# The token mixer of a two-block kernel, rewritten as a pipeline of dense steps with attention, index and recurrent groups between their units

## The chip, the cores and the metric

The kernel runs on one core of one Trainium2 chip, as one program. A core has a matrix engine (PE, TensorE, whose weight loads stand apart as PEld), a vector engine (DVE), a scalar engine (ACT), GpSimd (POOL) and a queue engine (SP) that here only issues weight transfers. The engines run side by side, each takes its own instructions in order, and they wait for one another on semaphores. The metric is device microseconds of one execution, as the median of the runs. Times inside the program are counted from the first instruction of the profiled execution.

## The reference, cut to what matters

Two transformer blocks run one after the other on 256 tokens of width 1024, all in float32. The change touches only the `token_mixer` of the second block:

```
proj = xn @ w_in
(qa, ka, va, qb, kb, vb, qi, ki, wi, xc, yc, gates) = split(proj)
y_a = moba_attention(qa, ka, va)            # causal softmax attention, 8 heads of 64, with a distance bias
y_b = dsa_attention(qb, kb, vb, qi, ki, wi) # the same, over the 64 keys that the index scores pick
y_c = rg_lru(causal_depthwise_conv(xc, conv_w, conv_b), ...) * gelu(yc)
g = sigmoid(gates).reshape(B, S, 3, D)
merged = g[:, :, 0] * (y_a @ w_pa) + g[:, :, 1] * (y_b @ w_pb) + g[:, :, 2] * (y_c @ w_pc)
return merged @ w_o
```

The index scores are `sum_h wi[h] * relu(qi[h] . ki)` over 8 heads, and a query keeps its 64 best keys. After the mixer come a residual sum, a norm and an MLP.

## The kernel before

**Dense steps.** Each weight matrix is worked off in steps. A step is 4 units (`SLOTS`) of 256 rows by 512 columns of the weight, 512 KB each. SP loads a unit into `raw`. ACT rounds it to `wh` (L1377), and DVE makes the rest `wl = raw - wh` (L2014). PE then makes three products for each tile (`three`, L550 to L554: high by high, high by low, low by high). `unit_used` counts the units that PE is done with, `lo_done` those that DVE has ready. A step "f" writes features by tokens (192 matmuls for two steps of 256 columns each way), a step "t" tokens by features. So while PE works on one step, ACT and DVE prepare the next one, unit by unit, each unit after PE has let go of its slot.

**PSUM in two halves.** Every step, and every group of small matmuls, takes the next half of PSUM (4 of 8 banks) by `open_group`, which waits until the half was emptied two groups ago (`emptied`, ticked by a one-element memset on DVE, L2036). So a small group between two steps has to be read out before the step after the next group can start.

**The mixer's order on PE** (L1243 to L1349): the steps qa, ka, va, qb, kb, vb, qi, kw (only 72 columns: ki and wi), xc, yc, then the transposition of the keys (L1256), gate step 0, the recurrence's gates (L1266), the index scores (L1279) with gate step 1 between their two tiles, and then the attention. It has four rounds n: 0 and 1 are the two halves of the heads of the first attention, 2 and 3 those of the second. A round is: scores (L1293), bias, mask and row maxima on DVE (`maxima`, L2726), exponentials on ACT (`softmax`, L1929), division on DVE (`normalise`, L2748), transposition of the probabilities on PE (L1303 to L1305), copies by ACT and DVE, product with the values (L1321). One gate step stands in each round. After the rounds come three steps `w_pa`, `w_pb`, `w_pc` (L1338 on), each multiplied by its gates on DVE (L2787) and summed (L2790), then 16 transposes of the sum (L1345), and two steps of `w_o`.

**DVE's own work** in the mixer: the weighted sum of the index scores (L2688 to L2695, 8 heads for each tile), the choice of the 64 best in two halves of four rounds (`choose`, L2719 to L2722), the convolution (L2661), the recurrent scan (L2708), the biases, maxima and divisions. The order on each engine is written out by hand: DVE and ACT call `split()` for all four units of the next step, then read out the step that just ended (`read_half`, `read_values`, `take_gate`).

ACT holds one table of functions at a time. Going from an exponential to a sigmoid or back is an ACT_TABLE_LOAD in its row of instructions.

Of the kernel before, what the change touches and what calls it, by code (L numbers as in the profile page):

```python
# [176 lines left out]
def build(nc, a, out):  # L177
    ctx = ExitStack()
    with ctx:
# [109 lines left out]
        rt, it = area(45, 4, SEQ), area(49, 4, SEQ)  # L289
        la, lt = area(53, 4, SEQ), area(57, 4, SEQ)  # L290
        wri = area(61, 2, 4, 64)
# [3 lines left out]
        gates3 = [area(kb, 2, 2, 512) for kb in (63, 37, 71)]  # L295
# [111 lines left out]
        merged = sem("merged")  # L407
        gain_loaded, out_ready = sem("gain_loaded"), sem("out_ready")
# [13 lines left out]
        def _(sp):  # L422
# [90 lines left out]
            with sp.Fori(0, 7) as i:  # L513
                S.enter(i, 1)
                load(cols(w, i * 512))
            S.leave(7)
            load(cols(w, W2["kw"], 72))
            with sp.Fori(0, 8) as i:
                S.enter(i, 1)
                load(cols(w, i * 512 + W2["xc"]))  # L520
            S.leave(8)
# [17 lines left out]
        def _(pe):  # L539
# [703 lines left out]
            for n, kind in enumerate("fftfftf"):  # L1243
                if kind == "f":
                    step_features(SEQ, fresh=n == 0)
                else:
                    step_tokens(range(2))
            step_tokens(range(2), 72)
            keys = G.now()
            step_features(SEQ)  # L1250
            conv = G.now()
            step_features(SEQ)
            pe.wait_ge(emptied, keys)
            hb = open_group()
            for t in range(2):
                mm = pe.transpose(ps[:, hb, t * P:(t + 1) * P], ki2[:, t, :], ident[:, :])  # L1256
            mm.then_inc(turned, 1)
            keys = G.now()
            step_tokens(range(2))
            pe.wait_ge(mix_loaded, 64)  # L1260
            pe.wait_ge(emptied, conv)
            hb = open_group()
            for z in range(2):
                for b in range(8):
                    r, m = slice(64 * (b % 2), 64 * (b % 2) + 64), b // 2
                    mm = pe.matmul(ps[r, hb + 2 * z + m // 2, (m % 2) * SEQ:(m % 2 + 1) * SEQ], wri[r, z, m, :],  # L1266
                                   xcv[r, m, :], start=True, stop=True)
            mm.then_inc(turned, 1)
# [4 lines left out]
            pe.wait_ge(emptied, keys)  # L1273
            for t, n in ((1, SEQ), (0, P)):
                hb = open_group()
                for h in range(8):
                    r, m = head_rows(h)
                    c = ((h % 2) * 4 + h // 2) * n
                    mm = pe.matmul(ps[:, hb + c // 512, c % 512:c % 512 + n], qkt5[r, 4, m, t * P:(t + 1) * P],  # L1279
                                   kit[r, 0:n], start=True, stop=True)  # L1280
                mm.then_inc(turned, 1)
                if t == 1:
                    step_tokens(range(2))

            def attend_scores(n):

                z, g = n // 2, n % 2
                hb = open_group()
                for t, bank, n in ((1, 0, SEQ), (0, 2, P)):
                    for x in range(4):  # L1290
                        r, m = head_rows(4 * g + x)
                        i = x // 2
                        mm = pe.matmul(ps[:, hb + bank + x % 2, i * n:(i + 1) * n], qkt5[r, 2 * z, m, t * P:(t + 1) * P],  # L1293
                                       qkt5[r, 2 * z + 1, m, 0:n], start=True, stop=True)
                mm.then_inc(turned, 1)

            def turn_probabilities(n):
                pe.wait_ge(prob_ready, n + 1)
                e = lg[:, n % 2, :]
                hb = open_group()  # L1300
                for x in range(4):
                    o = (x % 2) * SEQ
                    pe.transpose(ps[:, hb + x // 2, o:o + P], e[:, 1024 + x * P:1024 + (x + 1) * P], ident[:, :])  # L1303
# [22 lines left out]
            for n in range(4):  # L1326
# [3 lines left out]
                if n < 3:  # L1330
                    attend_scores(n + 1)
# [29 lines left out]
        def _(act):  # L1361
# [532 lines left out]
            def take_gate(c):  # L1894
# [3 lines left out]
                if c == 2:  # L1898
                    act.wait_ge(yc_lo, 1)
# [1094 lines left out]
```

## Time and profile before

| | us |
|---|---|
| median of 3 runs | 1985.83 (1985.02 to 1987.39) |
| the profiled execution, its own time | 1985.14 |
| its span, first to last instruction | 1983.3 |
| mixer, first dense matmul to the last of `w_o` | 1466.7 to 1779.0 |
| of it, PE without a matmul | 38.6 |

The profile's page gives busy time of each engine, the windows give it for a stretch, and the waits say which engine a waiting instruction was released by. A busy PE is not PE at full pace: the granted clock stands at either 2.4 GHz (1.00 in the rows) or 1.2 GHz (0.50), and a stretch that mixes both shows a number between. A wait on `spare` (L2036) is a wait for the memset that DVE ticks once a PSUM half has been read out by ACT and DVE.

### The profile page before, as it was taken

Reading aid. Unit: us, or ns where it says so; the run is one execution under the profiler, and the core shown is the slowest. Engines: PE = TensorE matmul, PEld = TensorE weight load, DVE = VectorE, ACT = ScalarE, POOL = GpSimd, SP = SyncE. Lnnn points to the kernel's source line nnn. Section 1 sums busy time; section 2 is a strip of 40 time slices with the busy share of each in tenths; the row PEclk is TensorE's granted clock in tenths of the full one; section 3 lists DMA queues with packets and bytes.
Section 4 is the critical chain, followed back from the end, with each engine's and each line's share of the span. In section 5 each row is a group of like instructions: output and inputs, shape, how many; then the busy total and the mean of one; then the engine's idle time right before and its main releaser. Section 6 shows DMA issues by size and latency. Waiting matters only on the chain.

```text
span 1983.3 us, 27192 instructions
## 1 busy us (share of the span) xinstructions
PE 1861.8 (94%) x10365; PEld 1527.3 (77%) x10365; DVE 962.5 (49%) x1375; ACT 848.6 (43%) x1216; POOL 108.4 (5%) x176
## 2 busy tenths in 40 slices
PE   4999999999999999999999997899999987979997
PEld 2776776767678877788878886899889966769986
DVE  2533423233257633334446564566655478545554
ACT  2423233233356522223335555566554366434453
POOL 3011111011100011000000000000010000000000
PEclk9999999999999999999999999899999889989999
DMA  9444444444455365332323222355555533436663
GB/s 311 135 144 130 137 152 128 151 127 144 137 183 199 118 210 168 109 96 77 115 72 108 75 88 83 123 185 180 192 169 164 172 96 130 136 96 180 180 191 106
DMA packets 151295, 282.43 MB, mean 142 GB/s; under 512 B 13027, under 2 KB 78683, under 8 KB 151072
## 3 DMA queue, kind: packets, MB, share of 16 engines
q1 hardware_dynamic: 133344, 220.54, 35.1%
q0 software_dynamic: 17856, 60.56, 9.5%
q8 instruction: 67, 1.10, 0.2%
q14 instruction: 28, 0.23, 0.0%
HBM read 276.83 MB, written 4.23 MB: 142 GB/s over the span
## 4 chain that ended last, share of the span: by engine, by line
PE 84%; DVE 6%; ACT 4%; DMA 3%; issue 2%; POOL 0%; SPq 0%; DVEq 0%; ACTq 0%
PE ps L552 24%; PE ps L553 23%; PE ps L554 23%; PE ps L805 3%; PE ps L597 2%; DMA raw<-in_ada_w 1%; PE ps L798 1%; DVE wl L2014 1%; ACT wh L1377 1%; DMA arena<-in_norm_g 1%; PE ps L692 1%; PE ps L1100 1%; PE ps L1081 1%; DMA arena<-in_ada_w 1%; PE ps L705 0%
## 5 line engine op out<-in xcount | busy, mean ns | idle before, releaser
L2014 DVE TENSOR_TENSOR wl<-raw,wh 128x1024 fp32r<-128x1024 f32 (+1 forms) x388 | 454.4, 1181 | 661.4 <-ACT wh L1377 659.6
L1377 ACT ACTIVATE wh<-raw 128x1024 fp32r<-128x1024 f32 (+1 forms) x388 | 393.6, 1023 | 761.6 <-PE ps L554 745.3
L552 PE MATMUL ps<-uh,wh 128*128 128x256 f32 (+1 forms) x1216 | 383.4, 315 | 7.3 <-DVE spare L2036 7.3
L552 PE MATMUL ps<-wh,uh 128*128 128x512 f32 (+2 forms) x960 | 363.7, 379 | 20.9 <-DVE spare L2036 7.7
L553 PE MATMUL ps<-ul,wh 128*128 128x256 f32 (+1 forms) x1216 | 381.2, 313 | 0.0
L554 PE MATMUL ps<-uh,wl 128*128 128x256 f32 (+1 forms) x1216 | 380.7, 313 | 0.0
L553 PE MATMUL ps<-wl,uh 128*128 128x512 f32 (+2 forms) x960 | 356.0, 371 | 0.0
L554 PE MATMUL ps<-wh,ul 128*128 128x512 f32 (+2 forms) x960 | 355.0, 370 | 0.0
L552 PEld LDWEIGHTS ps<-uh,wh 128*128 128x128 f32 x1216 | 235.2, 193 | 25.2 <-issue 10.6
L554 PEld LDWEIGHTS ps<-uh,wl 128*128 128x128 f32 x1216 | 234.9, 193 | 12.9
L553 PEld LDWEIGHTS ps<-ul,wh 128*128 128x128 f32 x1216 | 235.2, 193 | 12.3
L552 PEld LDWEIGHTS ps<-wh,uh 128*128 128x128 f32 x960 | 183.3, 191 | 76.2 <-issue 32.6
L552 PE MATMUL ps<-wh,ah 128*128 128x512 f32 x584 | 230.1, 394 | 2.6 <-DVE al L2569 1.7
L553 PE MATMUL ps<-wl,ah 128*128 128x512 f32 x584 | 228.0, 390 | 0.0
L554 PE MATMUL ps<-wh,al 128*128 128x512 f32 x584 | 228.0, 390 | 0.0
L554 PEld LDWEIGHTS ps<-wh,ul 128*128 128x128 f32 x960 | 183.4, 191 | 31.3
L553 PEld LDWEIGHTS ps<-wl,uh 128*128 128x128 f32 x960 | 183.6, 191 | 28.4
L552 PEld LDWEIGHTS ps<-wh,ah 128*128 128x128 f32 x584 | 110.4, 189 | 28.4 <-issue 4.7
L554 PEld LDWEIGHTS ps<-wh,al 128*128 128x128 f32 x584 | 110.0, 188 | 23.1
L553 PEld LDWEIGHTS ps<-wl,ah 128*128 128x128 f32 x584 | 110.3, 189 | 22.7 <-issue 0.2
L2905 POOL DMA_DIRECT2D arena<-in_ada_w x80 | 57.2, 717 | 549.5 <-PE ps L597 542.4
L805 PE MATMUL ps<-res,arena 128*128 128x512 f32 x160 | 71.5, 593 | 2.4 <-DVE spare L2036 2.3
(292 smaller groups left out, 1528.9 us busy)
## 6 DMA issues: line engine op xcount, KB each, us to landing
raw<-in_ffn_w_up SPq DMA_DIRECT2D x176, 256.0 KB
arena<-in_ada_w POOLq DMA_DIRECT2D x80, 512.0 KB, 4.9
raw<-in_w_in SPq DMA_DIRECT2D x60, 512.0 KB
raw<-in_ret_w_in SPq DMA_DIRECT2D x48, 512.0 KB
raw<-in_ffn_w_down SPq DMA_DIRECT2D x40, 512.0 KB
raw<-in_ret_w_out SPq DMA_DIRECT2D x32, 512.0 KB
raw<-in_w_up SPq DMA_DIRECT2D x32, 512.0 KB
raw<-in_w_down SPq DMA_DIRECT2D x32, 512.0 KB
```

Of the source, the lines that this page charges most:

```text
L552: pe.matmul(o, lh, rh, start=first, stop=False)
L553: pe.matmul(o, lh, rl, start=False, stop=False)
L554: return pe.matmul(o, ll, rh, start=False, stop=last)
L597: mm = pe.matmul(ps[q:q + 32, bank, 0:256], c32[:, 2 * u + kk, :], src[:, kk * 512 + cc * 256:kk * 512 + (cc + 1) * 256], start=u == 0, st ...
L692: pe.matmul(o, ident[:, :], ident[:, :], start=True, stop=True)
L798: mm = pe.matmul(o, qkt[:, 2 + f, k * P:(k + 1) * P], qkt[:, f, 0:n], start=f == 0, stop=f == 1)
L805: mm = pe.matmul(ps[:, half + t % 2, :], v0[:, c:c + P], vres[:, k, :], start=n == 0, stop=n == len(reads[t]) - 1)
L1081: mm = pe.matmul(ps[:, b + c, :], dqt[r, h, t * P:(t + 1) * P], dkt[r, h, :], start=True, stop=True)
L1100: mm = pe.matmul(ps[:, heads_v + h, t * P:(t + 1) * P], dpt[:, h, k, t * P:(t + 1) * P], dvs[i % 2][:, k, h * P:(h + 1) * P], start=k == 0 ...
L1377: T.mark(act.activation(wh[:, j, 0:size], raw[:, j, 0:size], ACT.Copy), hi_done)
L2014: T.mark(vec.tensor_tensor(wl[:, j, 0:size], raw[:, j, 0:size], wh[:, j, 0:size], ALU.subtract), lo_done)
L2905: pool.dma_start(aring[:, m % 2, :].rearrange("p (k n) -> p k n", k=2), w[u][:, :, c * 512:c * 512 + 512]).then_inc(ada_loaded[m % 2], 16)
```

## The change

Nothing of the arithmetic changes but one thing: the order in which the third branch is added. What moves:

- **Order of steps.** qa, ka, va, xc, qi, kw, yc, qb, kb, vb, then the six gate steps, `w_pa`, `w_pb`, `w_pc` and `w_o`. SP loads in that order, without a loop.
- **Groups between units.** A generator `mix_step` hands out the other half of PSUM after each unit, and the small groups are issued there: scores 0 in xc; scores 1 and the turned probabilities 0 in qi; values 0 in kw; keys, turned 1 and values 1 in yc; index scores in qb; scores 2 in gate step 0; scores 3 and turned 2 in gate step 1; values 2 and turned 3 in gate step 2; values 3 and the recurrence's gates in gate step 3. Each group has a semaphore pair of its own in place of `turned` and `emptied`. Before the first group of a step PE waits in `other_emptied` for the readout of the step before, and before the next step for the readout of the groups.
- **ACT and DVE** split the next step's units one by one (`parts`) with the mixer's work between them. The four exponentials of the wide rows and those of the narrow rows stand on two sides of a readout.
- **Convolution** reads a copy `xcp` of the step xc in SBUF and stands in gate step 2. `choose(False)` stands in kb, `choose(True)` in vb.
- **The tail.** The third branch's products come one token tile after the other (`rows_by_tile`). DVE multiplies, adds and hands on tile 0 while PE works on tile 1. The 16 transposes become 8 and 8, inside the step `w_pc` and inside the first step of `w_o`.
- The recurrence's buffers and the gates' buffers lie elsewhere in the arena, and the small recurrent weights in `rows`.

```diff
+            def mix_step(kind, n=512, fresh=False):
+
+
+                g = G.next()
+                half = 4 * (g % 2)
+                pe.wait_ge(emptied, g - 1)
+                for j in units(fresh):
...
+                    mm.then_inc(unit_used, 1)
+                    yield j, 4 - half
+
+            def other_emptied():
+
+                pe.wait_ge(emptied, G.now() - 1)
...
+            for j, o in mix_step("f"):
+                if j == 0:
+                    other_emptied()
+                    turn_keys(o)
+                elif j == 1:
+                    pe.wait_ge(keys_ready, 1)
+                    turn_probabilities(1, o)
+                elif j == 2:
+                    attend_values(1, o + 3)
+            pe.wait_ge(yab_lo, 2)
...
+            for j, o in mix_step("t"):
+                if j == 0:
+                    other_emptied()
+                    attend_scores(2, o)
+            pe.wait_ge(mix_taken, 3)
+            for j, o in mix_step("t"):
+                if j == 0:
+                    other_emptied()
+                    attend_scores(3, o)
+                elif j == 2:
+                    pe.wait_ge(mix_taken, 4)
+                    turn_probabilities(2, o)
+            pts_taken(3)
+            for j, o in mix_step("t"):
+                if j == 0:
+                    other_emptied()
+                    attend_values(2, o + 3)
+                elif j == 2:
+                    turn_probabilities(3, o)
+            pts_taken(4)
...
+            def turn_merged(t, half):
+
+                pe.wait_ge(merged, t + 1)
+                for f in range(KD):
...
+                mm.then_inc(mg_turned, 1)
...
+            for t, j in rows_by_tile(half, ctx_h, ctx_l, 0, True, True, pc_rows):
+                if (t, j) == (1, 1):
+                    other_emptied()
+                    turn_merged(0, 4 - half)
...
+            for t, j in rows_by_tile(half, ctx_h, ctx_l, 0, True, False, wo_rows):
+                if (t, j) == (0, 1):
+                    turn_merged(1, 4 - half)
+                elif (t, j) == (0, 3):
+                    pe.wait_ge(mg_lo, 2)
```

On ACT (`softmax(n, wide)` is the four wide or the four narrow exponentials):

```diff
+            parts(0, 1, 2)
+            softmax(2, True)
+            read_gate(0)
+            softmax(2, False)
+            parts(3)
+            parts(0, 1, 2)
+            softmax(3, True)
+            take_turned(2, even)
+            read_gate(1)
+            softmax(3, False)
+            parts(3)
```

On DVE:

```diff
+            parts(3)
+            parts(0, 1)
+            choose(True)
+            parts(2)
+            read_values(vab[:, 3, :])
+            parts(3)
+            parts(0)
+            biased(2, odd)
+            maxima(2)
+            parts(1, 2)
+            take_step()
+            parts(3)
+            parts(0)
+            biased(3, even)
+            parts(1)
+            normalise(2)
+            maxima(3)
+            parts(2)
+            take_turned(2, even)
+            take_step()
+            parts(3)
+            parts(0)
+            take_values(2, odd + 3)
+            normalise(3)
+            parts(1)
+            convolve()
+            parts(2)
+            take_turned(3, odd)
+            take_step()
```

How the engines' rows stand. On ACT before, around the exponentials of round 2 and the gate step behind them (`wh<-raw` is the rounding of a unit, `arena<-ps 128x2x512` the gate's readout):

```order
L1935 ACT_TABLE_LOAD
L1935 ACTIVATE arena,st<-arena,st 128x256 [waits nmax_ready]
L1935 ACTIVATE arena,st<-arena,st 128x256 x3
L1935 ACTIVATE arena,st<-arena,st 128x128 x4
L1377 ACTIVATE wh<-raw 128x1024 [waits unit_used,raw_loaded0]
```

The exponentials of a round stand in one piece, ahead of all four units of the next step. On ACT in the changed kernel, in gate step 1 (L2005 exponentials, L2011 the copy of the turned probabilities, L1996 the gate's readout, L1502 the rounding):

```order
L2005 ACTIVATE arena,st<-arena,st 128x256 [waits nmax_ready]
L2005 ACTIVATE arena,st<-arena,st 128x256 x3
L2011 ACTIVATE arena<-ps 128x1024 [waits prob_turned]
L1996 ACT_TABLE_LOAD [waits unit_used]
L1996 ACTIVATE arena<-ps 128x2x512 [waits pts_act]
L2005 ACT_TABLE_LOAD
L2005 ACTIVATE arena,st<-arena,st 128x128 x4
L1502 ACTIVATE wh<-raw 128x1024 [waits unit_used,raw_loaded3]
```

The copy of round 2's probabilities moved behind round 3's wide exponentials, and the fourth unit of the next step behind the readout and the narrow ones. On DVE before, at the end of the second half of the choice and the division of round 1 behind it:

```order
L2763 TENSOR_SCALAR arena<-arena 128x256 [waits vec_own]
L2763 TENSOR_SCALAR arena<-arena 128x128
L2753 RECIPROCAL st<-st 128x8 [waits exp_done]
L2754 TENSOR_TENSOR arena<-arena,st 128x1024 [waits vec_own]
L2755 TENSOR_TENSOR arena<-arena,st 128x512
```

On DVE in the changed kernel, the same end of the choice and what stands behind it (L2203 the low part of a unit, L2822 the readout of step vb, L2225 the tick of `emptied`, L2856 and L2858 the biased scores of round 2):

```order
L2842 TENSOR_SCALAR arena<-arena 128x256 [waits vec_own]
L2842 TENSOR_SCALAR arena<-arena 128x128
L2203 TENSOR_TENSOR wl<-raw,wh 128x1024 [waits hi_done]
L2822 COPY res<-ps 128x512 [waits unit_used,lo_done]
L2225 MEMSET spare 1x1 [waits vec_own,act_evac]
L2203 TENSOR_TENSOR wl<-raw,wh 128x1024 [waits hi_done] x2
L2856 SCALAR_TENSOR_TENSOR arena<-ps,arena 128x1024 [waits z_loaded0,mix_scored]
L2858 SCALAR_TENSOR_TENSOR arena<-ps,arena 128x512
```

The choice moved from inside the attention rounds to between two units of a dense step, and the readout of that step stands behind it.

## Rows read from the trace of the kernel before

**Rows 1.** The page: span, and busy time of PE and DVE.

```profile
span 1983.3 us, 27192 instructions
PE 1861.8 (94%) x10365; PEld 1527.3 (77%) x10365; DVE 962.5 (49%) x1375; ACT 848.6 (43%) x1216; POOL 108.4 (5%) x176
```

**Rows 2.** Windows: stretch, length, busy by engine, clock, DMA share, GB/s.

```profile
1466.70:1779.00 312.30, 273.71 (x1603) 237.47 (x1604) 183.54 (x263) 148.13 (x208) 8.70 (x13) 0.92 0.44 139
1466.70:1489.90 23.20, 23.17 (x193) 23.17 (x194) 12.14 (x15) 9.83 (x12) 5.87 (x9) 1.00 0.69 223
1489.90:1500.80 10.90, 10.90 (x50) 9.00 (x50) 5.65 (x6) 4.84 (x5) 0.00 (x0) 1.00 0.62 188
1546.20:1552.40 6.20, 6.20 (x51) 6.20 (x49) 4.40 (x6) 4.10 (x5) 0.00 (x0) 0.86 0.60 176
1552.30:1577.70 25.40, 25.40 (x194) 25.40 (x195) 14.73 (x22) 10.75 (x14) 0.00 (x0) 0.90 0.54 163
...
1644.40:1646.00 1.60, 1.54 (x18) 1.33 (x18) 0.75 (x3) 0.00 (x0) 0.00 (x0) 1.00 0.99 365
1646.00:1647.50 1.50, 1.49 (x18) 0.95 (x16) 1.36 (x2) 0.00 (x0) 0.00 (x0) 1.00 1.04 391
1659.10:1660.50 1.40, 1.40 (x13) 1.23 (x11) 1.40 (x2) 1.08 (x2) 0.00 (x0) 1.00 0.00 0
```

**Rows 3.** Waits of PE in 1466.7 to 1789: us in total, times, longest.

```profile
PE ps L1293 <- DVE spare L2036: 10.1, 4, 2.9
PE ps L552 <- DVE spare L2036: 9.8, 7, 3.6
PE ps L1345 <- DVE arena L2790: 7.1, 1, 7.1
PE ps L1303 <- DVE arena L2755: 5.5, 1, 5.5
PE ps L552 <- DVE ul L2793: 4.4, 1, 4.4
```

**Rows 4.** PE by line in the mixer: busy us, mean ns, idle before.

```profile
L1266 PE MATMUL ps<-arena 64*64 64x256 f32 x32 | 3.7, 379 | 0.0
L1279 PE MATMUL ps<-arena 64*128 64x256 f32 (+1 forms) x32 | 3.2, 336 | 0.3 <-DVE spare L2036 0.3
```

**Rows 5.** DVE by line and form, 1577.7 to 1747.

```profile
L2014 DVE TENSOR_TENSOR wl<-raw,wh 128x1024 fp32r<-128x1024 f32 x38 | 45.1, 1221 | 23.2 <-ACT wh L1377 23.2
...
L2733 DVE SCALAR_TENSOR_TENSOR arena<-ps,arena 128x1024 f32<-128x1024 f32 x4 | 4.9, 1224 | 5.1 <-PE ps L1293 5.1
L2745 DVE TENSOR_REDUCE st<-arena 128x4 f32<-128x1024 f32 x4 | 4.9, 1217 | 0.2
...
L2755 DVE TENSOR_TENSOR arena<-arena,st 128x512 f32<-128x512 f32 x4 | 2.7, 685 | 0.0
```

**Rows 6.** DVE in three windows: index sum, half a choice, convolution.

```profile
1604.00:1608.20 4.20, 3.85 (x9) 1.00 0.00 0
...
1631.80:1637.60 5.80, 5.49 (x25) 1.00 0.26 85
1569.60:1574.70 5.10, 4.99 (x13) 1.00 0.37 106
```

**Rows 7.** ACT by line and form, 1577.7 to 1747.

```profile
L1377 ACT ACTIVATE wh<-raw 128x1024 fp32r<-128x1024 f32 x37 | 38.2, 1054 | 41.2 <-PE ps L554 41.2
L1935 ACT ACTIVATE arena<-arena,st 128x256 f32<-128x256 f32 x16 | 7.9, 498 | 8.0 <-DVE st L2746 8.0
L1902 ACT ACT_TABLE_LOAD x6 | 7.7, 1283 | 0.1
L1935 ACT ACTIVATE arena<-arena,st 128x128 f32<-128x128 f32 x16 | 6.2, 387 | 0.0
...
L1944 ACT ACTIVATE arena<-ps 128x1024 f32<-128x1024 f32 x4 | 4.1, 1023 | 1.1 <-PE ps L1305 1.1
```

**Rows 8.** Timeline of ACT: start, length, and idle before in brackets.

```profile
1577.93 1.06 ACT L1377 ACTIVATE wh<-raw 128x1024 fp32r<-128x1024 f32 x1 [1.81 <-PE ps L554]
1579.00 1.28 ACT L1893 ACT_TABLE_LOAD   x1
1580.29 1.02 ACT L1893 ACTIVATE arena<-ps 128x1024 f32<-128x1024 f32 x1
```

More of the change, by code:

```diff
@@ L1240, in _ @@
             turn_normed(2)
[L1243 to L1267, printed above, removed]
@@ L1349, in _ @@
+            for _ in rows_by_tile(half, ctx_h, ctx_l, 4, False, True, rows_done):
+                pass
             turn_normed(2)
@@ L1866, in _, with parts @@
+            def parts(*order):
+                for u in order:
+                    split(units=range(u, u + 1))
+            mix0 = par.base
+            even, odd = 4 * (mix0 % 2), 4 - 4 * (mix0 % 2)
             split()
@@ L1951, in _ @@
-            for _ in range(3):
-                split()
-                S.next()
-                par.next()
-            hb = group_full()
-            T.mark(act.activation(uh[:, :, SEQ:TOK], ps[:, hb:hb + 4, :].rearrange("p b (x n) -> p (b x) n", x=2), ACT.Copy), act_evac)
+            split()
+            split()
+            S.base += 3
+            par.base += 2
+            half = 4 * (par.base % 2)
+            parts(0, 1)
+            take_merged(0, 4 - half)
+            parts(2, 3)
@@ L1957, in _ @@
+            take_merged(1, 4 - half)
+            par.base += 2
             split()
@@ new lines, in take_step, with parts @@
+            def take_step():
+                step_full()
+                close()
+            def parts(*order):
+                for u in order:
+                    split(units=range(u, u + 1))
+            mix0 = par.base
+            even, odd = 4 * (mix0 % 2), 4 - 4 * (mix0 % 2)
+            split()
+            read_half(qkt5[:, 0])
+            split()
+            read_half(qkt5[:, 1])
+            split()
+            read_values(vab[:, 1, :])
+            parts(0)
+            biased(0, even)
@@ new lines, in _ @@
+            maxima(0)
+            parts(1, 2)
+            take_step()
+            parts(3)
+            split(144, units=range(0, 1))
+            biased(1, odd)
+            normalise(0)
+            maxima(1)
+            split(144, units=range(1, 3))
+            take_turned(0, odd)
+            read_half(qkt5[:, 4])
+            split(144, units=range(3, 4))
+            parts(0, 1)
+            take_values(0, even + 3)
+            parts(2)
+            hb = step_full()
+            act_read()
```

627 lines of the change are left out of this document (381 added, 246 removed).

## The prediction

> **What bounds the kernel now.** First the page [rows 1]: PE is busy 94% of the span, so time can only be won where PE stands idle or runs slowly. Then the windows [rows 2]. The mixer is 312.3 us long, PE has a matmul in 273.7 of them, and the mean granted clock is 0.92. So 38.6 us are idle, and part of the busy time ran at 1.2 GHz.
>
> The waits [rows 3] say why it stands idle. Scores wait for a PSUM half to be ticked free (L1293, 10.1 us in 4 waits), dense steps likewise (9.8, with 2.1 just ahead of the mixer), the transposes of the merged sum wait for two DVE passes over 2048 columns (7.1) and `w_o` for the split of the result (4.4), the first probabilities for bias, maxima, four rounds of the choice and the division (5.5). All are hand-overs PE to DVE or ACT and back, with nothing else for PE to do.
>
> How much of the 273.7 is the slow clock? I build the mixer from rows at clock 1.00. Two f steps take 23.2 us, a t step 10.9, kw 6.2 [rows 2]. There are 7 f steps (81.2), 8 t steps (87.2), kw, three branch steps and two of `w_o` of t's shape (54.5): 229.1. Small groups: scores 1.5, values 1.5, turned probabilities 1.3 [rows 2], four times each, 17.2; recurrence 3.7 and index 3.2 [rows 4]; keys and merged sum 18 transposes at a twelfth of 1.3, 2.0. Sum 255.2. So 273.7 - 255.2 = 18.5 us are the price of the low clock. Where it comes from is seen behind kw: the next two f steps take 25.4 in place of 23.2 [rows 2], though PE never idled there. Kw's 48 matmuls of 72 columns were all it did before. Elsewhere the low stretches follow the waits.
>
> **What the change can win at most** is 38.6 + 18.5 = 57 us, all waits and all slow clock. Nothing is removed from any engine; one copy of 1.0 us on ACT is added and the convolution reads SBUF in place of PSUM. The nearest rows for that are DVE passes of 1024 columns, 1.22 us from PSUM (L2733) and 1.22 us from SBUF (L2745) [rows 5], so I take no difference; it is also off the path but for the place below. No transfer is added, and the weights are asked for when a unit is split, as before.
>
> **What stays as waits.** I go through the changed order by hand with durations from rows: a dense unit is a quarter of a step (2.9 f, 2.7 t), rounding it 1.05 on ACT [rows 7], its low part 1.22 on DVE [rows 5]; bias 1.9, maxima 1.9, with the mask 3.8, division 2.1 (passes of 1024 and 512 columns, 1.22 and 0.69, and a reciprocal of 0.2) [rows 5]; wide exponentials 4 x 0.5 = 2.0, narrow 4 x 0.39 = 1.55, table load 1.28, copy 1.02 [rows 7]; index sum 4.2, half a choice 5.8, convolution 5.1 [rows 6].
>
> In xc to yc the queues keep up. The readout of va is late by 0.3. In yc the probabilities of round 1 are wanted 3.2 us into the first two units, and DVE reaches their division only after a unit and the key copy: 1.7 late. Sum 2.0.
>
> In qb, kb, vb DVE has 12 units (14.7), the index sums (4.2 + 3.2), two half choices with the mask (12.1) and three readouts (2.5): 36.7 us, where PE has 23.2 + 10.9 + 3.2 = 37.3. DVE becomes as full as PE, and whatever stands behind it is late. Time 0 is now the start of gate step 0.
>
> - Second choice on DVE from -2.2 to 4.1, a unit to 5.3, the readout of vb to 6.2. PE is at `other_emptied` from 2.7: **3.5**.
> - Scores 2 end at 7.7, the step at 15.9. DVE has bias and masked maxima by 14.4. ACT then runs table load, wide exponentials (17.7), table load, gate readout (20.0), table load, narrow exponentials and the fourth unit (23.9; low part 25.1). PE wants the readout at 18.6: **1.4**.
> - Gate step 1: scores 3 to 21.5, two units to 27.0. DVE needs after 25.1 a unit, bias 3, a unit and division 2, to 31.5: **4.5**. Turned and last unit to 35.5. But ACT's copy of these probabilities stands behind the wide exponentials of round 3, which wait for maxima 3 at 35.3: done at 38.4: **2.9**.
> - Gate step 2 from 38.4: values 2 and units to 48.1. Behind two table loads and the narrow exponentials DVE gets its unit at 45.8, then a unit, values 2, division 3 to 49.7: **1.6**. Then a unit and the convolution (5.1), a unit and the copy of the turned probabilities to 57.9, where PE was through at 53.8: **4.1**.
>
> These are 18.0 us. From gate step 3 on the recurrence has slack. At the tail `w_pb`'s first unit on ACT stands behind a copy that waits for the scan: 1.9. The first merged tile comes 1.0 after two units of tile 1, the second 1.5 after the second unit of `w_o`: 4.4 in all, in place of 7.1 + 4.4 and slow transposes.
>
> **The sum.** 255.2 + 2.0 + 18.0 + 4.4 = 279.6. For the low clock I take 2.2 behind kw, which stays, and three more falls after the longest waits at 1.0 to 1.7 each (bounds: none, since DVE, not PE, sets the pace there; or all of today's 18.5), together 6. For some 20 hand-overs of 0.1 on the path another 2. That makes 287.6 in place of 312.3: 24.7 less. The profiled execution took 1985.1, within 0.7 of the median 1985.8; the forecast is 1985.8 - 24.7 = 1961.
>
> **A rule against the trace.** A table load lasts 1.28 us, and in the timeline it starts at the end of the instruction before and the next one starts 0.01 after it [rows 8]. The Trainium skill, ScalarE: Activation LUTs, section What ACT_TABLE_LOAD costs, says that a switch also drains the engine for about 1.38 us, 2.66 us in all. The trace doesn't show this.
>
> **Rivals.**
>
> - *Choked by DVE and ACT (the gain halves).* My hand schedule gives every instruction its place on time. If the queues from qb to gate step 3 slip by one unit (2.3 us for both engines) at each of five more places, 12 us go: **1973**. For it: DVE was busy 12.1 of 23.2 us even with plain steps [rows 2]. Against it: DVE idled 23.2 us waiting for ACT in the old attention part [rows 5], which the new order fills.
> - *Dear table switches.* Were a switch to hold ACT longer than its row, six switches lie on the path from gate step 0 to 2. With the one duration again for each, 6 x 1.28 = 8 us: **1969**. Against it rows 8. The rule of the Trainium skill, ScalarE: Activation LUTs, section What ACT_TABLE_LOAD costs, would do this; by its figure it is an estimate of 8.3.
> - *The clock falls more often.* Small groups now stand in nine dense steps. If each pulls the clock down as kw does, 2.2 us each, 20 us less 6 counted: **1975**. Against it: the window of turned probabilities ran at 1.00 [rows 2].
> - *Cheaper than I think.* If PE's waits at gate steps 0 to 2 overlap and clock losses vanish, half of the 18 and all of the 6 go: **1946**.
> - *Slower than before: the readout deadline.* Before, a PSUM half had a whole step (10.9) to be read out; now PE stands at `other_emptied` after one unit (2.7), in nine steps, and again before each next step for the groups' readouts. The readout stands behind whatever ACT and DVE are at. With ordinary readouts (1.0 to 1.3 after the step) it fits. If it came a unit and a choice (7 us) late in most of nine steps, 9 x 5.5 = 50 us come on top of the 255.2 + 24.4 + 8 + the lost overlap: 2010. It decides from a mean wait above 2.7 us more in nine steps. Only the one place behind the second choice has such a load ahead of it. I give it little.
>
> **How the numbers follow.** Forecast (1953 to 1967) 0.50, choked 0.18, table switches 0.03, clock 0.07, cheaper 0.12, about nothing gained 0.03, slower 0.07. Most likely time 1961. The range takes the forecast and its neighbours: 1944 to 1977. A measurement tells about 0.2%, 4 us, from no change. Faster 0.90, same 0.03, slower 0.07.
>
> **What would show it.** In the profile after: a mixer of some 288 us with PE idle about 25 us, more than half of it from gate step 0 to the end of gate step 2, on DVE's low parts, divisions and copies. No wait over 2 us in qa to kb. The tail without the 7.1 and 4.4. Kw still followed by a clock under 1.00. I would be wrong if PE waited long already in xc to yc (the deadline), if ACT rather than DVE released most waits, or if anything outside the mixer moved.

## The result, and the profile of the changed kernel

The changed kernel took 1960.87 us in the median of 4 runs (1957.94 to 1964.14), the kernel before beside it 1986.14 (1985.02 to 1987.39). The ratio is 0.9875, with an interval of 0.9859 to 0.9891. The forecast was 1961, in a range of 1944 to 1977. The profiled execution took 1959.8 us. The page, against [rows 1]:

```profile
span 1958.0 us, 27046 instructions
PE 1853.6 (95%) x10365; PEld 1517.7 (78%) x10365; DVE 961.0 (49%) x1373; ACT 846.7 (43%) x1217; POOL 108.7 (6%) x176
```

The span is 25.3 us shorter. DVE and ACT are as busy as before, as they have to be where nothing was removed. PE is busy 8.2 us less with the same 10365 matmuls: more of them ran at the higher clock.

Windows, with the columns of [rows 2]: the mixer, the first two f steps, kw with values 0, and the stretch behind it (yc, qb and the first 3 us of kb).

```profile
1466.30:1753.70 287.40, 265.12 (x1602) 228.01 (x1602) 181.86 (x261) 146.11 (x209) 8.73 (x13) 0.97 0.49 151
1466.30:1489.40 23.10, 23.10 (x192) 23.10 (x193) 12.08 (x15) 9.77 (x12) 5.88 (x9) 1.00 0.68 223
1528.60:1535.40 6.80, 6.80 (x66) 6.29 (x64) 4.02 (x6) 6.06 (x16) 0.00 (x0) 1.00 0.50 142
1535.40:1569.90 34.50, 32.73 (x280) 31.11 (x280) 20.27 (x31) 16.98 (x19) 0.00 (x0) 1.00 0.50 153
```

The mixer is 287.4 us long in place of 312.3, so the whole gain lies in it. From the end of `w_o` (1779.0 and 1753.7) to the end of the program it is 204.3 us in both. Inside, PE is without a matmul for 287.4 - 265.1 = 22.3 us in place of 38.6, and its busy time fell by 8.6. So 16.3 of the 24.9 us are waits and 8.6 are work done at a higher clock. The stretch behind kw has a clock of 1.00, where [rows 2] shows 0.90.

What PE waits for in the mixer, against [rows 3] (total, times, longest). L1311 is the wait of the scores (`other_emptied`), L1321 that of the turned probabilities, L1448 that of the merged sum's transposes, and L559 is the first matmul of a unit. The one put down to "issue" is the wait ahead of gate step 3, for DVE's copy of the last turned probabilities (L2889).

```profile
PE ps L1321 <- DVE arena L2884: 6.7, 3, 3.8
PE ps L1311 <- DVE spare L2225: 5.5, 3, 3.2
PE ps L559 <- issue: 3.8, 1, 3.8
PE ps L1448 <- DVE arena L3061: 3.3, 2, 1.7
PE ps L559 <- DVE wl L2203: 2.2, 1, 2.2
PE ps L559 <- DVE spare L2225: 2.1, 1, 2.1
PE ps L559 <- ACT arena L2011: 0.8, 1, 0.8
```

The 2.1 of `spare` at L559 lies just ahead of the mixer, as before. The rest sums to 22.3. The waits of 7.1 and 4.4 at the tail are gone.

The attention part reads differently. First the stretch with PE's longest waits, from the start of step vb to some 5 us into gate step 3, then the one around the wait of the scores of round 2:

```profile
1578.60:1655.00 76.40, 61.93 (x278) 48.43 (x276) 53.08 (x99) 38.96 (x63) 0.00 (x0) 0.89 0.42 128
1593.00:1610.00 17.00, 14.46 (x61) 11.78 (x62) 12.50 (x16) 5.95 (x12) 0.00 (x0) 0.80 0.44 133
```

PE lacks 14.5 us here, more than half of the mixer's 22.3, at a clock of 0.89. Neither DVE (53.1 of 76.4) nor ACT (39.0) is full. They wait for each other. What DVE waits for in the window from 1578 to 1655 (total, times, longest):

```profile
DVE spare L2225 <- ACT arena L1996: 9.4, 3, 4.7
DVE wl L2203 <- ACT wh L1502: 9.4, 4, 3.7
```

DVE stands still 18.8 us for ACT, for a gate's readout (L1996) and for a rounded unit (L1502). ACT in gate step 1, its timeline (start, length, and idle before in brackets):

```profile
1627.39 0.52 ACT L2005 ACTIVATE arena<-arena,st 128x256 f32<-128x256 f32 x1 [6.25 <-DVE st L2875]
...
1629.38 1.00 ACT L2011 ACTIVATE arena<-ps 128x1024 f32<-128x1024 f32 x1
1630.39 1.28 ACT L1996 ACT_TABLE_LOAD   x1
1631.69 1.03 ACT L1996 ACTIVATE arena<-ps 128x1024 f32<-128x1024 f32 x1
1632.73 1.28 ACT L2005 ACT_TABLE_LOAD   x1
...
1635.58 2.00 ACT L1502 ACTIVATE wh<-raw 128x1024 fp32r<-128x1024 f32 x2
```

ACT waits 6.25 us for DVE's maxima. Only then come the exponentials, the copy, a table load, the readout and another table load, and the next unit's rounding stands behind all of them. That is one chain, DVE to ACT to DVE.

### The profile page after: what moved, and what is told of

The parts are those of the page before. It is cut to its first block, busy times and chain, and to the rows that moved or that the text cites. A ratio compares the mean times of both kernels' runs of the same rounds, so it can differ in the third digit from the quotient of the medians.

```text
span 1958.0 us, 27046 instructions
## 1 busy us (share of the span) xinstructions
PE 1853.6 (95%) x10365; PEld 1517.7 (78%) x10365; DVE 961.0 (49%) x1373; ACT 846.7 (43%) x1217; POOL 108.7 (6%) x176
## 4 chain that ended last, share of the span: by engine, by line
PE 83%; DVE 7%; ACT 4%; DMA 3%; issue 2%; POOL 0%; SPq 0%; ACTq 0%; DVEq 0%
PE ps L559 24%; PE ps L560 23%; PE ps L561 23%; PE ps L812 4%; PE ps L604 2%; DVE wl L2203 2%; DMA raw<-in_ada_w 2%; ACT wh L1502 1%; PE ps L805 1%; DMA arena<-in_ada_w 1%; DMA arena<-in_norm_g 1%; PE ps L1107 1%; PE ps L1088 1%; PE ps L699 1%; PE ps L712 1%
## 5 line engine op out<-in xcount | busy, mean ns | idle before, releaser
L2203 DVE TENSOR_TENSOR wl<-raw,wh 128x1024 fp32r<-128x1024 f32 (+1 forms) x388 | 454.6, 1182 | 643.8 <-ACT wh L1502 641.6
L1502 ACT ACTIVATE wh<-raw 128x1024 fp32r<-128x1024 f32 (+1 forms) x388 | 393.0, 1022 | 734.8 <-PE ps L561 715.4
L559 PE MATMUL ps<-uh,wh 128*128 128x256 f32 (+1 forms) x1216 | 382.3, 314 | 7.3 <-DVE spare L2225 7.3
L559 PE MATMUL ps<-wh,uh 128*128 128x512 f32 (+2 forms) x960 | 364.5, 380 | 13.3 <-issue 8.8
L559 PEld LDWEIGHTS ps<-uh,wh 128*128 128x128 f32 x1216 | 233.4, 192 | 26.2 <-issue 10.8
L559 PEld LDWEIGHTS ps<-wh,uh 128*128 128x128 f32 x960 | 183.4, 191 | 69.0 <-issue 37.9
L559 PE MATMUL ps<-wh,ah 128*128 128x512 f32 x584 | 230.4, 394 | 4.8 <-DVE wl L2203 2.2
L559 PEld LDWEIGHTS ps<-wh,ah 128*128 128x128 f32 x584 | 110.5, 189 | 30.6 <-issue 6.8
```

Of the source, the lines that this page charges most:

```text
L559: pe.matmul(o, lh, rh, start=first, stop=False)
L1502: T.mark(act.activation(wh[:, j, 0:size], raw[:, j, 0:size], ACT.Copy), hi_done)
L2203: T.mark(vec.tensor_tensor(wl[:, j, 0:size], raw[:, j, 0:size], wh[:, j, 0:size], ALU.subtract), lo_done)
```

## The experiments

The changed kernel's four times lie up to 6 us apart (1957.94 to 1964.14). In the traces of all kernels here the mixer starts anywhere from 1465.8 to 1470.2, though nothing ahead of it was changed. So I compare the length of the mixer in each trace, and beside it how long the granted clock was low in it.

| kernel | mixer us | PE busy | low clock us | time us |
|---|---|---|---|---|
| before | 312.3 | 273.7 | 47.8 | 1986.14 |
| changed | 287.4 | 265.1 | 17.1 | 1960.87 |
| changed, once more (e12) | 287.5 | 263.7 | 13.7 | 1959.10 |
| old tail (e1) | 300.4 | 268.3 | 27.3 | 1970.28 |
| no second choice (e3) | 281.2 | 262.2 | 10.2 | 1953.14, single run |
| no tables in gate steps 0 and 1 (e4) | 280.9 | 263.6 | 13.7 | 1953.73, single run |
| no taps (e2) | 280.7 | 260.7 | 6.8 | 1956.85, single run |
| unit before scan (e7) | 285.3 | 263.6 | 13.7 | 1957.64 |
| kernel before, kw filled (e9) | 315.8 | 276.2 | 47.8 | 1988.29, single run |
| more DVE work early (e10) | 287.6 | 263.8 | 13.7 | 1961.49, single run |
| more DVE work late (e11) | 290.9 | 264.9 | 20.5 | 1963.12, single run |
| convolution early (e5) | 281.0 | 260.6 | 6.8 | 1953.72 |
| and copy first (e6) | 281.6 | 262.1 | 10.2 | 1954.66 |
| e5, e6 and e7 together (e8) | 278.0 | 260.6 | 6.8 | 1949.95 |

Columns three and four belong together. Among the kernels with the changed kernel's matmuls, PE's busy time is 260.6 at 6.8 us of low clock, 262.1 at 10.2, 263.7 at 13.7 and 265.1 at 17.1. One us of low clock costs 4.5 / 10.3 = 0.44 us of busy time. The line meets zero at 257.6, the busy time at full clock. It holds where PE mostly works while the clock is low (15.3 of 17.0 us in the changed kernel). In e11 it doesn't: 264.9 at 20.5 us, where the line gives 266.6. A low stretch of 10.2 us began there 4.8 us before the end of a wait of 7.0, so half of it met no work. E1, with the old tail, lies below the line too (268.3 at 27.3, where it gives 269.6).

### How the gain divides (e1)

The new pipeline, with the tail of the kernel before put back on PE, ACT and DVE:

```diff
-            for t, j in rows_by_tile(half, ctx_h, ctx_l, 0, True, True, pc_rows):
-                if (t, j) == (1, 1):
-                    other_emptied()
-                    turn_merged(0, 4 - half)
...
+            hb = open_group()
+            step_down(lambda t: hb + 2 * t, range(2), True, True, late=False, kt=0, src=(uh[:, :, SEQ:TOK], ul[:, :, SEQ:TOK]))
+            pe.wait_ge(merged, 1)
...
+            mm.then_inc(turned, 1)
+            all_emptied()
+            project(2, 2, late=False, src=(uh[:, :, SEQ:TOK], ul[:, :, SEQ:TOK]))
```

> The changed kernel with the old tail: the three branch steps, then 16 transposes of the whole sum, one copy and one split, then w_o. My theory (the tail is worth its waits and slow clock): PE waits of some 7.1 and 4.4 us come back in place of 1.6 and 1.7, and the low clock at the transposes and at the start of w_o with them, 2 to 3 us; the median is 9 to 12 us above the changed kernel's 1960.9, about 1971. Rival (the tail's waits only move into the norm behind it, so the gain is all from the pipeline): within 2 us of 1961.

Measured: 1970.28 us, a ratio to before of 0.9922 (0.9905 to 0.9938), so 9.4 above the changed kernel. PE's waits at the tail and the mixer's window:

```profile
PE ps L1464 <- DVE arena L3068: 7.1, 1, 7.1
PE ps L559 <- DVE ul L3071: 4.5, 1, 4.5
...
1468.70:1769.10 300.40, 268.25 (x1602) 231.16 (x1602) 181.58 (x257) 145.95 (x208) 8.73 (x13) 0.95 0.47 144
```

Both waits of [rows 3] are back to within a tenth, and 10.2 us of low clock (from 1735.0 and from 1745.2) come with them. In this trace the first two f steps took 24.8 in place of 23.1, about 1.5 of it by 3.4 us of low clock at the mixer's start. So 300.4 - 1.5 = 298.9 compares with 287.5: the tail is worth 11.4 us, 8.3 of it waits and the rest low clock. The pipeline ahead of it is worth 312.3 - 298.9 = 13.4. No run separates what in it is owed to the new order of steps and what to the groups between units.

### What the first long wait hangs on (e3, e10, e11)

In e3 the second choice of keys is left out, all but its bias and mask:

```diff
-                pick(TOPK // 16)
+                if not last:
+                    pick(TOPK // 16)
```

> The second four rounds of the choice of the 64 best keys are left out (5.5 us of DVE work in step vb); the rest is as changed. My theory (DVE is full from qb to vb and the readout of vb stands behind the choice): the wait of 3.2 us at scores 2 goes to under 0.5, the 6.8 us of low clock behind it too (worth 2 to 3), so 4 to 6 us less, about 1955 in one look; the waits of 1.8 and 3.8 in gate step 1 stay, since they hang on scores 2, not on the choice. Rival (what DVE no longer does late, ACT does late: one chain of latencies from gate step 0 on takes it all back): the waits in gate steps 0 to 2 grow by what the first one shrank, and the time stays within 1 us.

Measured: 1953.14 us, the mixer 6.2 shorter. PE's waits:

```profile
PE ps L1321 <- DVE arena L2885: 6.7, 3, 3.8
...
PE ps L1311 <- DVE spare L2225: 2.3, 2, 1.8
```

L1311 has lost its 3.2 and kept the 1.8 of the next gate step, and the turned probabilities wait as before. So without the choice ahead of vb's readout the 3.2 us are gone, and nothing of them comes back further on. The second half of the 6.2 is the clock: 17.1 - 10.2 = 6.9 us less of it low, at 0.44 these are 3.0.

In the next two kernels DVE makes the low part of some units twice, once into the same place for nothing. That adds 1.2 us of DVE work a unit; e10 does it for a whole step early in the mixer, e11 for the units around the second choice.

```diff
+                    if twice:
+                        own(vec.tensor_tensor(wl[:, j, 0:size], raw[:, j, 0:size], wh[:, j, 0:size], ALU.subtract))
...
             read_half(qkt5[:, 0])
-            split()
+            split(twice=True)
```

> The changed kernel, with the low part of each of the four units of the second f step, ka, worked out twice on DVE: 4 x 1.22 plus waits, 5.3 us more DVE work in the step where DVE is busy about half the time. My theory (PE sets the pace there): the mixer stays within 0.5 us of 287.5. Rival (any DVE work in the mixer counts): 5 us more.

Measured: 1961.49 us, the mixer 287.6 long, 0.1 more than in e12. DVE's busy time in it rose by 4.8 us (186.8 in place of 181.9). Early in the mixer it has slack for that.

```diff
-            parts(0, 1)
+            split(units=range(0, 1), twice=True)
+            split(units=range(1, 2), twice=True)
             choose(True)
-            parts(2)
+            split(units=range(2, 3), twice=True)
             read_values(vab[:, 3, :])
-            parts(3)
+            split(units=range(3, 4), twice=True)
```

> The same 5.3 us of doubled low parts, but for the four units that DVE prepares during step vb, where the second choice stands. My theory (DVE is full from qb to vb, and what it is late by PE waits at scores 2): three of the four are ahead of the readout of vb, so the wait of 3.2 us at scores 2 grows by 3.9 to about 7, the rest of the chain keeps its distances, and the mixer is 4 us longer (291.5), a little more or less by the clock. Rival (DVE had slack of several us there, and the wait at scores 2 is owed to something else): the mixer within 1 us of 287.5.

Measured: 1963.12 us, the mixer 3.5 longer. PE's waits:

```profile
PE ps L1311 <- DVE spare L2227: 9.3, 3, 7.0
PE ps L1321 <- DVE arena L2886: 6.7, 3, 3.8
```

The longest wait grew from 3.2 to 7.0, the ones behind it did not move. Of 4.8 us more DVE work three quarters stand ahead of vb's readout, and the mixer grew by 3.5. The same work costs nothing in one place and three quarters of its length in another.

### Table loads on the path (e4)

Gate steps 0 and 1 are read out by a plain copy in place of the sigmoid, so no table is changed there:

```diff
-                T.mark(act.activation(gates3[c // 2][:, :, c % 2, :], ps[:, hb:hb + 2, :], ACT.Sigmoid), act_evac)
+                T.mark(act.activation(gates3[c // 2][:, :, c % 2, :], ps[:, hb:hb + 2, :], ACT.Copy if c < 2 else ACT.Sigmoid), act_evac)
```

> The sigmoid of gate steps 0 and 1 is left out (a plain copy in its place), so that ACT needs no table load between the wide and the narrow exponentials of rounds 2 and 3: four loads of 1.28 us less, the rest as changed. My theory (these loads lie on the path): the gate readout in gate step 0 comes 1.3 earlier and the fourth unit 2.6 earlier, so the wait of 1.8 at scores 3 falls to about 0.5, the wait of 3.8 at the turned probabilities to about 1.3, and the wait at turned probabilities 3 (1.1) to 0; 4 us less, about 1956. Rival (DVE alone sets the pace there): none of these waits falls by more than 0.5.

Measured: 1953.73 us, the mixer 6.5 shorter. PE's waits:

```profile
PE ps L1311 <- DVE spare L2225: 4.2, 3, 3.2
PE ps L1321 <- DVE arena L2884: 4.2, 2, 2.4
PE ps L559 <- issue: 2.7, 1, 2.7
```

Three totals fell, 5.5 to 4.2, 6.7 to 4.2 and 3.8 to 2.7, in all 4.9 us. With 3.4 us less of low clock (1.5) that accounts for the 6.5. The expectation of 4 counted waits only, and not all of them rightly: the wait at turned probabilities 2 fell from 3.8 to 2.4, not to 1.3, and the one ahead of gate step 3 fell by 1.1, which I had left out. The loads are on the path, at the 1.28 us that the timeline shows for each. ACT has four instructions fewer than in the changed kernel, 205 in place of 209, and four loads at 1.28 are 5.1. A second duration for each would have let the waits fall by up to 10. That speaks against a hidden cost, without excluding it, since another engine may be the next to be late. The timeline above has the next instruction 0.02 us after the load's end.

### The convolution and its wait (e2, e5, e6)

In e2 the three taps of the convolution are left out:

```diff
-                for d in (1, 2, 3):
...
+                tick(xcv_ready)
```

> The three delayed taps of the convolution are left out (5.0 us of DVE work in gate step 2); the rest is as changed. My theory: the wait of 3.8 us ahead of gate step 3 goes to 0 and so does the low clock of 6.8 us behind it (2 to 3 us), 5 to 7 us less than the changed kernel, about 1955. Rival (the copy of the turned probabilities is late for another reason, ACT's gate readout): the wait stays above 2 us.

Measured: 1956.85 us, the mixer 6.7 shorter (280.7). The time is only 4.0 below the changed kernel's, since the mixer starts at 1470.1 in this trace and at 1466.3 in the other. The wait of 3.8 ahead of gate step 3 is gone, and so is the low clock that followed it. DVE's timeline in the changed kernel shows what stood in its place:

```profile
1641.51 1.22 DVE L2203 TENSOR_TENSOR wl<-raw,wh 128x1024 fp32r<-128x1024 f32 x1
1642.85 5.07 DVE L2919 SCALAR_TENSOR_TENSOR arena<-arena,gcol 128x255 f32<-128x255 f32 x12
1647.83 1.22 DVE L2203 TENSOR_TENSOR wl<-raw,wh 128x1024 fp32r<-128x1024 f32 x1
1648.97 0.68 DVE L2889 COPY arena<-ps 128x512 f32<-128x512 f32 x1
```

PE waits for the last of these lines. The convolution's input, the step xc, was ready more than 100 us earlier. So e5 keeps all the work and only moves it to yc and qb:

```diff
             take_values(1, odd + 3)
+            convolve(1, 2)
             take_step()
             parts(3)
+            convolve(3)
...
             parts(1)
-            convolve()
             parts(2)
```

> The changed kernel with the convolution moved, nothing left out: its first two taps on DVE behind the low part of values 1 in step yc, the third behind the fourth unit there, where DVE otherwise waits, in place of gate step 2. My theory: the wait of 3.8 us ahead of gate step 3 and the low clock behind it go (worth 6.8 where the taps were left out), and DVE is 1 to 2.5 us later into the full stretch from qb on, so the mixer is 4 to 6 us shorter, about 282.5, median about 1956. Rival (the load only moves: DVE, full from qb on, hands the 5 us on to the wait at scores 2): the mixer within 1.5 us of 287.5.

Measured: 1953.72 us, a ratio to before of 0.9834 (0.9817 to 0.9851), with a mixer 6.5 shorter than e12's, which ran on the same chip. PE's waits:

```profile
PE ps L1311 <- DVE spare L2225: 5.5, 3, 3.2
...
PE ps L559 <- ACT arena L2011: 2.4, 1, 2.4
...
PE ps L1343 <- DVE spare L2225: 0.4, 1, 0.4
```

The scores' 3.2 did not grow: what was put ahead of the second choice was not handed on to it. The 3.8 ahead of gate step 3 is gone, and values 3 in that step (L1343) now wait 0.4 for a readout. That is 3.4 us of wait, and 6.9 us less of low clock at 0.44 are 3.0, together 6.4.

The 2.4 on ACT's L2011 is the wait at the end of gate step 1. It is 0.8 in the changed kernel's first trace, e3, e4 and e11, and 2.4 in e12, e1, e2, e5, e7 and e10. Where it is 0.8, the unit ahead of it ran at the low clock and took 4.6 us in place of 3.0. PE came later, and nothing was won. In e6 the copy it waits for is put first:

```diff
             parts(0, 1, 2)
-            softmax(3, True)
             take_turned(2, even)
+            softmax(3, True)
             read_gate(1)
```

> The run before this one, and on ACT the copy of the turned probabilities 2 ahead of the wide exponentials of round 3. The wait it aims at was 0.8 us in the changed kernel, 2.4 where PE had no low clock ahead of it. My theory: that wait goes, but what comes next, division 3 in gate step 2, hangs on maxima 3 and the exponentials and not on PE, so its wait of 1.1 grows by as much: no more than 1 us shorter than with the convolution moved alone. Rival (PE's waits add up, each removed one counts): 2 us shorter.

Measured: 1954.66 us, 0.9838 (0.9818 to 0.9858), the mixer 281.6. The wait fell from 2.4 to 1.2 (put down to "issue" in this trace), and the next turned probabilities wait 0.3 more:

```profile
PE ps L1321 <- DVE arena L2884: 7.0, 3, 3.8
...
PE ps L559 <- issue: 1.2, 1, 1.2
```

By the waits that is 0.9 us of gain. The mixer is 0.6 longer all the same, since this trace has 3.4 us more of low clock, in `w_pb`. So this run alone can't tell whether the edit is worth anything. The trace of e8 below has it at the same 6.8 us of low clock as e5, and there it is worth 0.8.

### The tail's first unit (e7)

ACT rounds two units of `w_pb` ahead of the copy that waits for the recurrent scan:

```diff
             parts(3)
+            parts(0, 1)
             act.wait_ge(yc_ready, 1)
             T.mark(act.activation(uh[:, 0:4, SEQ:TOK], gy, ACT.Copy), yc_hi)
-            split()
+            parts(2, 3)
             split()
```

> The changed kernel, but on ACT the first two units of the step w_pb are rounded ahead of the copy that waits for the recurrent scan, and no longer behind it. My theory (the 2.2 us that PE waits at the start of w_pb is this one instruction's place in ACT's row): the wait goes to under 0.3 and the mixer is 2 us shorter (287.5 to 285.5). Rival (the third branch's operands, late by the same scan, or the tail behind it take the place): the tail's waits of 1.6 and 1.7 grow and the mixer stays within 0.5 us of 287.5. The median, about 1959, is within noise of the changed kernel's either way; the trace decides.

Measured: 1957.64 us, 0.9854 (0.9838 to 0.9870), with a mixer 2.2 shorter than e12's at the same length of low clock. The interval overlaps that of the changed kernel, so the trace has to decide, as expected. The wait of 2.2 for `wl` is gone, and the two behind it stay:

```profile
PE ps L1448 <- DVE arena L3062: 3.2, 2, 1.7
```

### The clock behind kw (e9)

This one starts from the kernel before. Sixteen float32 matmuls of 128 columns that nobody reads are put into the middle of kw (the trace records each of them twice, 32 in all):

```diff
+                if j == 1:
+                    keep_clock(ps[:, hb + 3, 384:TOK], 16)
```

> The kernel before, with 16 matmuls of 128 columns on a free bank between the second and the third unit of the 72-column step kw, 1.8 us of them; nothing else is moved. It stands in for the product with the values that the changed kernel puts there. In the kernel before, the clock falls to 1.2 GHz for 6.8 us behind kw and the next two f steps take 25.4 in place of 23.2; in the changed kernel it doesn't. Theory A (kw's own thin matmuls pull the clock down, and anything dense in their middle keeps it up): no low clock within 20 us behind kw, two f steps of 23.2. Theory B (the fall is a matter of when kw comes, or comes from what stands ahead of kw): a low stretch of 3.4 or 6.8 us stays behind kw.

Measured: 1988.29 us, the mixer 315.8. Kw with the filler, the two f steps behind it, the filler alone, and the mixer:

```profile
1545.80:1554.70 8.90, 8.90 (x83) 8.90 (x81) 3.51 (x5) 4.10 (x5) 0.00 (x0) 1.00 0.70 217
1554.70:1577.80 23.10, 23.10 (x195) 23.10 (x195) 15.50 (x22) 10.76 (x14) 0.00 (x0) 1.00 0.49 144
1548.40:1552.00 3.60, 3.60 (x34) 3.60 (x34) 2.45 (x2) 1.07 (x2) 0.00 (x0) 1.00 0.59 176
1466.30:1782.10 315.80, 276.16 (x1636) 239.33 (x1637) 183.55 (x264) 148.14 (x208) 8.71 (x13) 0.92 0.44 138
```

The two f steps take 23.1 at a clock of 1.00, where [rows 2] has 25.4 at 0.90. So theory A held in this one trace: the clock fell where kw's narrow matmuls stood alone, with PE never idle, and did not with wider ones among them. The filler takes 3.6 us, twice what I had expected. It saves 2.3 in the f steps and 0.8 in kw, which takes 8.9 - 3.6 = 5.3 without it and 6.1 in the kernel before, where the clock falls 4.4 us into it. The total of low clock stayed at 47.8 us: of the stretches behind the next three waits two were longer and one shorter (6.8, 6.8 and 10.2 us in place of 3.4, 10.2 and 3.4), and the mixer lost 3.5. What decides how long such a stretch lasts stays open. It can't be read from one trace.

### The three mended places together (e8, e12)

> Convolution early, copy first, and w_pb's first two units rounded ahead of the copy that waits for the scan. My theory: the sum of the three, mixer about 280, median 1953 to 1955, faster than the changed kernel by 0.3%. Rival (with gate step 3 earlier, the recurrence is late for the tail instead): mixer 283 or more.

> The changed kernel as it is, on the same chip as the three above, to compare them with. Expected at 1958 to 1964, mixer 287.5.

Measured side by side: e8 1949.95 us (1946.13 to 1954.22), a ratio to before of 0.9811 (0.9795 to 0.9828). The changed kernel again had 1959.10 (1956.32 to 1962.90), 0.9859 (0.9841 to 0.9878). The intervals don't meet, and e8 is 9.1 us below. It has the lowest median and the shortest mixer of all kernels here, 36.5 us below the kernel before on the same chip. I had expected 1953 to 1955 and a mixer of 280, so the three edits together gave more than I thought; e12 came as expected. The mixer and PE's waits in it:

```profile
1470.20:1748.20 278.00, 260.60 (x1602) 225.17 (x1602) 181.69 (x261) 146.29 (x209) 8.71 (x13) 0.99 0.51 156
...
PE ps L1321 <- DVE arena L2885: 7.0, 3, 3.8
PE ps L1311 <- DVE spare L2226: 5.5, 3, 3.2
...
PE ps L1448 <- DVE arena L3063: 3.2, 2, 1.7
PE ps L559 <- issue: 1.2, 1, 1.2
```

The mixer is 9.5 shorter than e12's; e5 and e7 alone make 6.5 + 2.2 = 8.7, and the copy's edit the other 0.8, as its waits say (2.4 to 1.2, less 0.3). What is left above 2 us are the second choice's 3.2 and the 3.8 of the turned probabilities, both on the chain of DVE and ACT.

## Why the prediction was right, point by point

**What bounds the kernel** held. The gain came from PE's idle time (16.3 us) and its low clock in the mixer, and nothing outside it moved. Of the signs that the prediction named, the length of the mixer, the idle time, its place (14.5 of 22.3 us between gate steps 0 and 2), qa to kb without a wait over 2 us and the tail came true. The clock behind kw did not.

**The waits, one by one.** Forecast and measured, in the order of the program:

| wait | forecast | measured |
|---|---|---|
| scores 0 in xc | 0.3 | 0.5 |
| turned 1 in yc | 1.7 | 1.8 |
| scores 2, gate step 0 | 3.5 | 3.2 |
| scores 3, behind gate step 0's readout | 1.4 | 1.8 |
| turned 2, gate step 1 | 4.5 | 3.8 |
| end of gate step 1 | 2.9 | 0.8 (2.4 at full clock) |
| turned 3, gate step 2 | 1.6 | 1.1 |
| ahead of gate step 3 | 4.1 | 3.8 |
| `w_pb` | 1.9 | 2.2 |
| merged tiles | 1.0 and 1.5 | 1.6 and 1.7 |
| sum | 24.4 | 22.3 |

Following the queues, with durations of single instructions, found every wait over 1 us. Only one is off by more than 0.7. The 2.9 assumed PE on time at the end of gate step 1; in this trace it came late by the slow clock.

**The base of 255.2** was too small by 2.4 for the changed kernel: the traces put its busy time at full clock at 257.6. For the kernel before it is nearly right. PE works in 37.3 of the 47.8 us of low clock there, and a us of such work costs about 0.47 (the 16 score matmuls of round 2 take 2.9 us at the low clock, those of round 3 take 1.5 at full clock). So 273.7 - 0.47 x 37.3 = 256.2 is an estimate of its work at full clock, and the new order added about 2 us of work to PE. In e8's trace, counted from the start of one matmul to that of the next and with the low clock taken off, the dense steps take some 227 us in place of the 222.9 in my sum. Kw and the small groups take about 2 less. A dense unit that a group stands ahead of is longer: yc's second unit took 3.1 us without its wait, an undisturbed f unit 2.9. One row was also misread. The prediction says that its rows are at clock 1.00, but kw's 6.2 stands in [rows 2] at 0.86. At full clock it is 5.4, two halves of 2.7.

**The clock's 6 us.** Of it 2.2 were to stand behind kw. They did not come: the clock is 1.00 there in the changed kernel, where values 0 stand between kw's units, as in e9 with filler between them. The low clock stood elsewhere, at 1594.5, 1625.2 and 1649.1, in all 17.1 us. At 0.44 these cost 7.5. The place was wrong and the price of the other falls too small (7.5 in place of 3.8). That the other falls come with a long wait was right: two begin within one (3.2 and 3.8 us), one 1.4 us behind the end of one (3.8). The reason I gave for the lower bound, that DVE and not PE sets the pace there so that a slow clock costs nothing, holds for one place alone, the end of gate step 1.

**The 2 us for hand-overs** don't exist as waits: all 22.3 us without a matmul are in the waits above. In size they are what the cut steps added to PE's work. That is another thing, and the sum put it at nothing. The sum, with what was measured: 257.6 + 22.3 + 7.5 = 287.4, against 255.2 + 24.4 + 6 + 2 = 287.6. Four terms were off, by +2.4, -2.1, +1.5 and -2.0, and the signs cancel. The forecast met the time to 0.1 us (1961 and 1960.87) by luck; by its terms it was good to about 3.

**The cost of the edits.** The convolution from SBUF took 5.07 us, from PSUM before 5.02, so no difference, as taken. The DVE was as busy as before.

**DVE or ACT.** The prediction said that it would be wrong if ACT released most waits. By name DVE released all but one. Behind it the engine that sets the pace changes: at the scores of round 2 it is DVE, full with the choice (e3, e11); from there to gate step 3 it is the chain of both, in which DVE itself waits 18.8 us for ACT and table loads lie on the path (e4). "Choked by DVE and ACT" as a rival asked for 12 us more and did not come. Its premise, that DVE is as full as PE, is true only until vb's readout: from 1561.4 to 1595.4 it was busy 32.3 of 34.0 us, from there to 1655 only 37.1 of 59.6.

**The table loads.** They were counted at 1.28 each on the path, and waits that rest on them came within 0.7 us. The rival by which each switch costs a second duration had these waits 8 us longer. The Trainium skill, ScalarE: Activation LUTs, section What ACT_TABLE_LOAD costs, names 2.66 us for a switch; here 1630.39 plus 1.28 is followed by 1631.69, and no drain is seen on either side.

**The readout deadline** did not decide. At `other_emptied` it costs 0.5, 3.2 and 1.8 us in three of nine steps, and ahead of the next step, for the copies of a group, 0.8 and 3.8 in two. E11 shows what it would do: 3.8 us more at the one step that a long block stands ahead of.

## What to carry to other kernels

When small groups are put between the units of a dense step, the time of a group's start is that of the readout ahead of it in the slowest queue. So no long block of vector work whose input is old may stand in front of a readout or of a copy that PE waits for. Moving 5 us of such work from gate step 2 back to yc and qb made the mixer 6.5 us shorter (the medians differ by 5.4), without a change in any instruction.

A wait of 3 to 4 us on PE cost 6 to 6.5 here (e3, e5), since the clock that fell with it cost another 3. Such waits are worth removing one by one, and the low-clock stretches in a trace point at them.

To forecast such a change, walk the queues from one common time: this found ten of eleven waits to within 0.7 us. Check each row's clock before it goes into a base, and add something for each place where a dense step is cut: here whole steps measured apart were about 4 us short in 20 of them.

## What the runs showed of the hardware

The busy time of PE rises with the time at low clock by 0.44 us for each us, over four values from 6.8 to 17.1 us. In e11, at 20.5 us, it did not rise further (264.9 and 265.1), since half of one low stretch fell into a wait. Two executions of one kernel differed in it, 17.1 and 13.7, at equal mixers (287.4 and 287.5), because the extra low stretch stood where PE would otherwise have waited for ACT's copy.

The clock fell 4.4 us into kw's 48 matmuls of 72 columns (6.8 us of it low) with PE never idle. It did not when 3.6 us of matmuls of 128 columns (e9, one trace), or the values of one attention round (1.5 us, every trace of the changed order), stood between them. I had not expected that removing this fall would leave the total of low clock as it was (47.8 us in the traces of the kernel before and of e9); why is open.
